# Low halves of the weights moved from GpSimd to VectorE, and the first two products behind four norms made row by row

## The chip, the cores and the metric

The kernel runs on one core of a Trainium2 chip. The time is device microseconds from start to end of one execution; the median of several runs is what two kernels are compared by. The profile is one further execution, recorded instruction by instruction. Engines are written as the profile writes them: PE is TensorE's matmuls, PEld its weight loads, DVE is VectorE, ACT is ScalarE, POOL is GpSimd, SP the queue that issues the DMAs.

## The reference, cut to what matters

Two blocks of two layers each, everything in fp32, 256 tokens of 1024 channels. The first block makes, in each layer, one wide input product and three branches (a Mamba-2 scan, a sliding-window attention, a forgetting attention), gates and adds them:

```
for layer in range(DEPTH):
    h = rms_norm(x, norm_w[layer])
    proj = jnp.einsum('bsd,de->bse', h, w_in[layer])
    ...
    x = x + jnp.einsum('bsd,de->bse', merged, w_out[layer])
return rms_norm(x, final_norm_w)
```

The second block has a second stream `xc` of 256 context tokens beside x, modulates each norm with a scale and a shift that come from a condition vector, and has a mixing half (attention, pooling, Fourier) and a feed-forward half:

```
h = modulate(rms_norm_2(x, norm_mix[l]), sh1, sc1)
... = jnp.split(h @ w_in[l], IN_SPLITS, axis=-1)
x = x + g1 * merge_branches(...)
hf = modulate(rms_norm_2(x, norm_ffn[l]), sh2, sc2)
x = x + g2 * conv_ffn(hf, w_up[l], conv_w[l], w_down[l])
```

In layer 0 of it both streams run (512 columns), in layer 1 the context stream needs only its keys and values.

## The kernel before

**An fp32 product as three products.** Each operand is split into a high part that PE takes exactly (`hi`, an ACT copy to fp32r) and a low part (`lo` = raw - hi). A product is hi·hi + hi·low + low·hi, three matmuls of 128x128 weights (lines 878 to 880 in `chan`, 891 to 893 in `toks` where the activations are the stationary side, 953 to 955 in `small`).

**The weights.** They stream from HBM by SP's queue in halves of 128x1024 into 7 buffers `raw`, and from there into a ring of 5 buffers `hi` and `lo` (`NS` = 5, line 15). A `split` of a half is two instructions: ACT makes `hi` (line 1239; it waits until PE has used the half five places back, `was("used", u.i - NS)`), then the subtraction makes `lo`, on DVE (line 1554) or on POOL (line 2021), after `hi`. Which one is decided in `plan`:

```
u.x = (w, len(rows), "dve" if u.i >= NS and u.i % (4 if u.x[0] else 2) == 1 else "pool")
```

The first flag of `u.x` is `self.share`: every second half goes to DVE in the forgetting-attention and convolution part of the first block, every fourth elsewhere, none of the first five.

**The order.** `Order` (line 196 on) writes one list of units by hand. Every engine walks through the same list and runs its own part of each unit in order, waiting on semaphores. `gemm` (line 265) makes a product of 8 rows k of 128 channels: `split_after(i, 0)` (the refill of the ring place that this product's first half frees), the product, `split_after(i, 1)`, then `tick`, which appends one step of each side work (attention, scan, mixing). A product of 256 columns by 256 tokens is 48 matmuls. In an `urgent` product the refills are put off: `early_split` and `late_splits` (lines 235 and 240) place them around the next norm.

**The norms.** A norm number t is: the squares on ACT summed on DVE into `t_SQA` (line 1564), a matmul with ones (916), a square root on ACT (1267), a reciprocal on DVE (1571), a matmul that spreads it over the partitions (923), and then the eight rows. In the first block (`norm1`) rows come in pairs: DVE scales into PSUM (1585), ACT copies to the high part (1278), DVE subtracts to the low part (1591). In the second block (`norm2`) per row: DVE (1850), for 512 columns DVE (1853) and ACT (1423), ACT makes the high part (1426), and the low part is made on DVE (1842) for even rows and on POOL (2051) for odd ones; in norms 3 and 8 on DVE for all. Each row of the product behind waits for its row of the norm, `at("h", u.l, k)`.

Norms and the first product behind each: 0 and 1 in the first block, `small` (128 columns) and then `q`; 3 in the second block's layer 0, `uf`; 4, the feed-forward of layer 0, `up`, one chunk whose two column groups of 128 by 512 tokens are two units; 5, layer 1, `uf` twice; 6, its feed-forward, `up` twice.

Of the kernel before, what the change touches and what calls it, by code (L numbers as in the profile page):

```python
# [144 lines left out]
class Unit:  # L145
# [9 lines left out]
    n: tuple = ()  # L155
    x: tuple = ()


class Order:
# [105 lines left out]
    def gemm(self, kind, l, c, fn, nkt, ncol, tw, urgent=False, x=(), then=None):  # L265
# [133 lines left out]
    def layer1(self, l):  # L399
# [11 lines left out]
        for g in range(4):  # L411
            for off, kind in ((O_QC, "q"), (O_KC, "k")):
# [89 lines left out]
    def block2(self, l):  # L502
# [67 lines left out]
        for pr in range(11):  # L570
            g, p2 = (pr + 1) // 2, (pr + 1) % 2
            for vg in range(2):
                self.gemm("up", l, pr, wcols("w_up_2", l, vg * DFF + np.arange(pr * 256, pr * 256 + 256)), 8, 256, tw,
                          x=(vg,), then=lambda m0: self.up_then(l, pr, vg, m0, tw))
# [267 lines left out]
def tensor(e, units, t, M):  # L842
# [25 lines left out]

    def chan(u, nkt, ncol, tw, xh, xl, point, *events):

        b = gbank(u)
        for k in range(nkt):
            q.wait_ge(point(k))
# [8 lines left out]

    def toks(u, nkt, ncol, c0, nc, xh, xl, blocks, point, part):

        b = gbank(u)
        for k in range(nkt):
            q.wait_ge(point(k))
            hi, lo = weights(u, k, ncol)
            for j, tb in enumerate(blocks):
# [54 lines left out]

    def of_h(u, *events):
        chan(u, 8, 256, 256, hh, hl, lambda k: at("h", u.l, k), *events)

    def small(u):
        b = gbank(u)
        for k in range(8):  # L950
            q.wait_ge(at("h", u.l, k))
# [127 lines left out]

    def uf(u):  # L1080
        z, nz = u.x
        toks(u, 8, 256, 0, 256, block(t.H2), block(t.HL2), (2 * z, 2 * z + 1),
             lambda k: at("h", 8 if u.l == 0 and z else 3 + 2 * u.l, k), z)

# [111 lines left out]
    todo = dict(rstd=rstd, rstdb=rstdb, mod=mod, mod2=mod2, q=of_h, k=of_h, conv=of_h, rope=of_h, z=of_h, gate=lambda u: of_h(u, ("gatemm", u.l)),  # L1196
                small=small, small4=small4, vc=vc, vb=vc, scores=scores, turn=turn, pv=pv, ssm0=ssm0, ssm3=ssm3, ssm4=ssm4,
                rope2=rope2, gn_sum=gn_sum, proj=proj, wout=wout, uf=uf, k2=k2, v2=v2, q2=lambda u: of_h2(u, 256 if u.l else 512),
                gate2=lambda u: of_h2(u, u.x[3]), rope2b=rope2b, pool1=pool1, four1=four1, mix2=mix2, pair0=pair0, pair3=pair3,
                pair4=pair4, proj2=proj2, wout2=wout2, up=ffup, down=down)  # L1200
    for u in units:
        if u.kind in todo:
            todo[u.kind](u)
# [333 lines left out]
def vector(e, units, t, M):  # L1537
# [296 lines left out]
    def norm2(u):  # L1834
# [175 lines left out]
def gpsimd(e, units, t, M):  # L2010
# [52 lines left out]
def plan():  # L2063
# [199 lines left out]
```

## Time and profile before

| | |
|---|---|
| median of 3 runs | 2189.99 us (2189.62 to 2190.36) |
| the profiled execution: its time, its span | 2188.52 us, 2186.8 us |
| PE busy | 2085.0 us, 95% |
| DVE busy | 1230.1 us, 56% |
| ACT busy | 1112.0 us, 51% |
| POOL busy | 959.3 us, 44% |
| `lo` on POOL, `lo` on DVE | 360 and 146 instructions |

The span is 1.7 us shorter than that execution's own time, and that time lies 1.5 us under the median of the runs. A matmul's record is longer than the step to the next one, since matmuls overlap; how fast PE goes is read from the steps between starts and from counts in a stretch. PE's granted clock is given as a share of its full rate: 1.00 is 2.4 GHz, 0.50 is 1.2 GHz.

### The profile page before, as it was taken

How to read it: one execution, taken by the hardware profiler on the slowest of the kernel's cores; microseconds unless marked ns; L12 is line 12 of the kernel's file. 1: busy time of each engine (PE TensorE's matmuls, PEld its weight loads, DVE VectorE, ACT ScalarE, POOL GpSimd, SP SyncE). 2: the span in 40 equal slices, each digit the busy share in tenths (PEclk: the TensorE clock that was granted, in tenths of full speed). 3: DMA queues.
4: the chain of work that ended last, by engine and by line, in shares of the span. 5: the costliest groups of instructions: out<-in, count | busy, mean ns of one | idle time of the engine just before them, and what ended most of it. 6: DMA issues, size and time to landing. Idle time of an engine off the chain costs nothing.

```text
span 2186.8 us, 36805 instructions
## 1 busy us (share of the span) xinstructions
PE 2085.0 (95%) x14870; PEld 1856.7 (85%) x14870; DVE 1230.1 (56%) x2034; ACT 1112.0 (51%) x1892; POOL 959.3 (44%) x424
## 2 busy tenths in 40 slices
PE   6999999999999999999999999999999989999997
PEld 6998998998898999988666876778888777898997
DVE  5577757345677655473464435455544546766565
ACT  5575476544585475554475233433333346645553
POOL 4655654653546555642112332323333233465662
PEclk9999999999999999999999999999999989999998
DMA  6454544565654544563212434333333333354551
GB/s 238 150 189 170 185 149 147 183 221 186 225 177 157 182 155 154 195 227 110 97 68 77 163 127 164 116 125 125 116 135 107 131 109 109 124 183 140 189 184 58
DMA packets 93321, 330.65 MB, mean 151 GB/s; under 512 B 10080, under 2 KB 13408, under 8 KB 92896
## 3 DMA queue, kind: packets, MB, share of 16 engines
q1 hardware_dynamic: 93152, 328.30, 43.6%
q8 instruction: 118, 1.93, 0.4%
q14 instruction: 51, 0.42, 0.1%
HBM read 327.08 MB, written 1.18 MB: 150 GB/s over the span
## 4 chain that ended last, share of the span: by engine, by line
PE 76%; DVE 11%; ACT 7%; issue 2%; DMA 2%; POOL 2%; SPq 0%; DVEq 0%; ACTq 0%; POOLq 0%
PE ps L878 21%; PE ps L879 21%; PE ps L880 21%; ACT t_hi L1239 2%; PE ps L932 2%; DVE t_lo L1554 1%; DMA t_A<-cu_scratch 1%; PE ps L891 1%; PE ps L892 1%; PE ps L893 1%; POOL t_lo L2021 1%; PE ps L1150 1%; DVE t_SQA L1564 1%; PE ps L1006 1%; PE ps L1160 1%
## 5 line engine op out<-in xcount | busy, mean ns | idle before, releaser
L2021 POOL TENSOR_TENSOR t_lo<-t_raw,t_hi 128x1024 fp32r<-128x1024 f32 (+1 forms) x360 | 884.9, 2468 | 1059.7 <-ACT t_hi L1239 1035.9
L878 PE MATMUL ps<-t_RB,t_hi 128*128 128x256 f32 (+1 forms) x3712 | 1170.8, 315 | 17.3 <-DVE t_RB L1842 5.3
L879 PE MATMUL ps<-t_RB,t_hi 128*128 128x256 f32 (+1 forms) x3712 | 1149.4, 310 | 0.0
L880 PE MATMUL ps<-t_RB,t_lo 128*128 128x256 f32 (+1 forms) x3712 | 1148.7, 309 | 0.0
L878 PEld LDWEIGHTS ps<-t_RB,t_hi 128*128 128x128 f32 x3712 | 712.3, 192 | 90.5 <-issue 31.5
L880 PEld LDWEIGHTS ps<-t_RB,t_lo 128*128 128x128 f32 x3712 | 712.6, 192 | 35.7
L879 PEld LDWEIGHTS ps<-t_RB,t_hi 128*128 128x128 f32 x3712 | 712.9, 192 | 34.9 <-issue 1.9
L1239 ACT ACTIVATE t_hi<-t_raw 128x1024 fp32r<-128x1024 f32 (+1 forms) x506 | 524.7, 1042 | 421.6 <-PE ps L880 387.9
L1554 DVE TENSOR_TENSOR t_lo<-t_raw,t_hi 128x1024 fp32r<-128x1024 f32 x146 | 211.2, 1447 | 264.4 <-ACT t_hi L1239 264.3
L1980 DVE SCALAR_TENSOR_TENSOR t_A<-ps,t_V,t_A 128x510 f32<-128x510 f32 (+1 forms) x176 | 102.2, 612 | 153.8 <-ACT t_A L1514 152.2
L1514 ACT ACTIVATE t_A<-ps,t_V 128x512 f32<-128x512 f32 (+1 forms) x88 | 48.5, 576 | 126.8 <-PE ps L880 126.8
L1953 DVE SCALAR_TENSOR_TENSOR t_X<-ps,t_MOD,t_X 128x256 f32<-128x256 f32 x168 | 72.1, 478 | 62.4 <-PE ps L880 62.4
L891 PE MATMUL ps<-t_hi,t_RB 128*128 128x256 f32 (+1 forms) x320 | 94.3, 295 | 4.3 <-DVE t_RB L1842 2.9
L892 PE MATMUL ps<-t_hi,t_RB 128*128 128x256 f32 (+1 forms) x320 | 91.5, 286 | 0.0
L893 PE MATMUL ps<-t_lo,t_RB 128*128 128x256 f32 (+1 forms) x320 | 91.5, 286 | 0.0
L891 PEld LDWEIGHTS ps<-t_hi,t_RB 128*128 128x128 f32 x320 | 62.9, 196 | 9.5 <-ACT t_E L1423 5.2
L1500 ACT ACTIVATE t_A<-ps 128x512 f32<-128x512 f32 (+1 forms) x48 | 22.4, 490 | 89.1 <-PE ps L880 85.9
L892 PEld LDWEIGHTS ps<-t_hi,t_RB 128*128 128x128 f32 x320 | 63.1, 197 | 0.4 <-issue 0.2
L893 PEld LDWEIGHTS ps<-t_lo,t_RB 128*128 128x128 f32 x320 | 63.0, 197 | 0.0
L1564 DVE TENSOR_TENSOR t_SQA<-t_SQA,t_NT 128x256 f32<-128x256 f32 (+1 forms) x63 | 47.5, 754 | 21.5 <-ACT t_NT L1260 18.0
L1526 ACT ACTIVATE t_RB<-t_A 128x512 fp32r<-128x512 f32 (+1 forms) x44 | 23.1, 526 | 70.5 <-DVE t_A L1995 70.5
L932 PE MATMUL ps<-t_raw,t_C 128*32 128x256 f32 x768 | 53.0, 399 | 2.6 <-DVE t_X L1953 2.6
(295 smaller groups left out, 2154.5 us busy)
## 6 DMA issues: line engine op xcount, KB each, us to landing
t_raw<-in_W SPq DMA_DIRECT2D x586, 512.0 KB, 3.5
t_A<-cu_scratch SPq DMA_DIRECT2D x8, 512.0 KB, 6.3
t_B<-cu_scratch SPq DMA_DIRECT2D x8, 512.0 KB, 4.4
t_raw<-in_W SPq DMA_DIRECT2D x16, 256.0 KB, 2.6
t_A<-in_C SPq DMA_DIRECT2D x2, 1536.0 KB, 6.8
t_X<-in_X SPq DMA_DIRECT2D x2, 512.0 KB, 4.4
t_X<-in_X SPq DMA_DIRECT2D x1, 1024.0 KB, 9.6
out<-t_X SPq DMA_DIRECT2D x1, 1024.0 KB, 4.8
```

The lines of the kernel that those rows point to most:

```text
L878: mm(o, hi[:, w], xh(k), start=k == 0 and j == 0, stop=False)
L879: mm(o, hi[:, w], xl(k), start=False, stop=False)
L880: i = mm(o, lo[:, w], xh(k), start=False, stop=k == nkt - 1 and m == u.x[1] - 1)
L891: mm(o, xh(k, tb), hi[:, w], start=k == 0 and j == 0, stop=False)
L892: mm(o, xl(k, tb), hi[:, w], start=False, stop=False)
L893: i = mm(o, xh(k, tb), lo[:, w], start=False, stop=k == nkt - 1 and tb == blocks[-1])
L932: i = mm(b[32 * j:32 * j + 32, 0:256], t.C32[:, k, :], t.raw[r % NR][:, j * 256:j * 256 + 256], start=k < 4, stop=k >= 4)
L1239: act(t.hi[s][:, 0:w], t.raw[r][:, 0:w], ACT.Copy).then_inc(*up("act", ("hi", u.i), ("split", u.i)))
L1554: tt(t.lo[s][:, 0:w], t.raw[r][:, 0:w], t.hi[s][:, 0:w].bitcast(F), ALU.subtract).then_inc(*up("dve", ("split", u.i)))
L1953: stt(out=x, in0=ps[:, z * 256:z * 256 + 256], scalar=t.modv(u.l, j, k, z), in1=x, op0=ALU.mult, op1=ALU.add).then_inc(*up("dve", ("x", s, ...
L1980: return stt(out=o[:, :, r], in0=ps[:, :, s], scalar=cw, in1=o[:, :, r], op0=ALU.mult, op1=ALU.add)
L2021: tt(t.lo[s][:, 0:w], t.raw[r][:, 0:w], t.hi[s][:, 0:w].bitcast(F), ALU.subtract).then_inc(*up("pool", ("split", u.i)))
```

## The change

Three edits. (1) `plan` sends every `lo` to DVE, all 506, the first five too; the low parts of all norm rows go to DVE, so POOL keeps only `fox_prep`, `ssm0` and `ssm2`. (2) A new `wide` unit takes the first two products behind norms 0, 1, 4, 5 and 6 and makes them row by row: for rows 0 to 5 first the one's matmuls, then the other's, and rows 6 and 7 at the end one after the other. Behind norms 0 and 1 these are `small` and `q` of group 0 (which stood one product later), behind 4 the two column groups of one `up` chunk, behind 5 the two `uf`, behind 6 the two `up`. The refills of the ring stand behind the `wide` unit. (3) In norms 5 and 6 one `early_split` more stands ahead of the reciprocal.

```
+    def wide(self, l, parts, tw):
+        group, chunks = [], []
+        for kind, c, fn, ncol, x, then in parts:
+            i = self.chunk(8 * ncol, fn)
...
+        self.add("wide", l=l, x=tuple(u for u, _, _ in group))
+        halves = [(i, h) for i in chunks for h in range(-(-self.width[i] // HF))]
+        self.split_after(*halves.pop(0))
+        for u, then, m0 in group:
...
+            self.units.append(u)
+            if halves:
+                self.split_after(*halves.pop(0))
@@ small
-        i = self.chunk(1024, small_cols(l))
-        self.split_after(i, 0)
-        self.add("small", l=l, i=i, g=(self.bank(),))
-        self.split_after(i, 1)
+        self.wide(l, [("small", 0, small_cols(l), 128, lambda m: (), None),
+                      ("q", 0, wcols("w_in", l, O_QC + np.arange(256)), 256, lambda m: (0, 2), None)], 256)
@@ block2, norm 5 (norm 6: if last)
+            self.early_split()
             b = self.rstd(t, (2, 1, 1))
@@ tensor
+    def wide(u):
+        for k in range(6):
+            for v in u.x:
+                led[v.kind](v, ks=(k,))
+        for v in u.x:
+            led[v.kind](v, ks=(6, 7))
@@ vector, norm2
-            if k % 2 == 0 or s in (3, 8):
+            if True:
@@ gpsimd, norm2
-        if s in (3, 8):
-            return
+        return
@@ plan
-            u.x = (w, len(rows), "dve" if u.i >= NS and u.i % (4 if u.x[0] else 2) == 1 else "pool")
+            u.x = (w, len(rows), "dve")
```

**DVE at norm 0**, the start of the program. Before:

```order
4 L1571 RECIPROCAL t_SM<-t_SM 128x2
5 L1585 SCALAR_TENSOR_TENSOR ps<-t_X,t_V,ps 128x256 x4
6 L1591 TENSOR_TENSOR t_RB<-ps,t_RB 128x512
7 L1585 SCALAR_TENSOR_TENSOR ps<-t_X,t_V,ps 128x256 x2
8 L1591 TENSOR_TENSOR t_RB<-ps,t_RB 128x512
9 L1585 SCALAR_TENSOR_TENSOR ps<-t_X,t_V,ps 128x256 x2
10 L1591 TENSOR_TENSOR t_RB<-ps,t_RB 128x512 x2
```

and now (lines of the new file stand 38 higher: 1592 is the `lo` subtraction, 1609 the reciprocal, 1623 and 1629 the norm's rows):

```order
4 L1592 TENSOR_TENSOR t_lo<-t_raw,t_hi 128x1024
5 L1609 RECIPROCAL t_SM<-t_SM 128x2
6 L1623 SCALAR_TENSOR_TENSOR ps<-t_X,t_V,ps 128x256 x4
7 L1629 TENSOR_TENSOR t_RB<-ps,t_RB 128x512
8 L1592 TENSOR_TENSOR t_lo<-t_raw,t_hi 128x1024
9 L1623 SCALAR_TENSOR_TENSOR ps<-t_X,t_V,ps 128x256 x2
10 L1629 TENSOR_TENSOR t_RB<-ps,t_RB 128x512
11 L1592 TENSOR_TENSOR t_lo<-t_raw,t_hi 128x1024
12 L1623 SCALAR_TENSOR_TENSOR ps<-t_X,t_V,ps 128x256 x2
13 L1629 TENSOR_TENSOR t_RB<-ps,t_RB 128x512
14 L1592 TENSOR_TENSOR t_lo<-t_raw,t_hi 128x1024
```

One `lo` stands ahead of the reciprocal now, and one between each two pairs of rows.

**PE behind norm 0.** Before, the last two rows k of `small` (953 to 955) and the first of `q`:

```order
21 L953 MATMUL ps<-t_RB,t_hi 128x256
22 L954 MATMUL ps<-t_RB,t_hi 128x256
23 L955 MATMUL ps<-t_RB,t_lo 128x256
24 L953 MATMUL ps<-t_RB,t_hi 128x256
25 L954 MATMUL ps<-t_RB,t_hi 128x256
26 L955 MATMUL ps<-t_RB,t_lo 128x256
27 L878 MATMUL ps<-t_RB,t_hi 128x256
28 L879 MATMUL ps<-t_RB,t_hi 128x256
29 L880 MATMUL ps<-t_RB,t_lo 128x256
```

and now, from the first row on (990 to 992 are `small`, 907 to 909 are `q`):

```order
3 L990 MATMUL ps<-t_RB,t_hi 128x256
4 L991 MATMUL ps<-t_RB,t_hi 128x256
5 L992 MATMUL ps<-t_RB,t_lo 128x256
6 L907 MATMUL ps<-t_RB,t_hi 128x256
7 L908 MATMUL ps<-t_RB,t_hi 128x256
8 L909 MATMUL ps<-t_RB,t_lo 128x256
9 L907 MATMUL ps<-t_RB,t_hi 128x256
10 L908 MATMUL ps<-t_RB,t_hi 128x256
11 L909 MATMUL ps<-t_RB,t_lo 128x256
12 L990 MATMUL ps<-t_RB,t_hi 128x256
```

Each row of the norm now feeds nine matmuls before PE asks for the next.

**DVE at norm 6**, the last feed-forward. Before:

```order
1478 L1564 TENSOR_TENSOR t_SQA<-t_SQA,t_NT 128x256 x2
1479 L1830 TENSOR_SCALAR t_S1S<-t_MOD 128x16
1480 L1832 TENSOR_TENSOR t_S1S<-t_S1S,t_V 128x16
1481 L1571 RECIPROCAL t_SM<-t_SM 128x2
1482 L1575 TENSOR_TENSOR t_RS<-t_C,t_SM 128x256
```

and now:

```order
1714 L1602 TENSOR_TENSOR t_SQA<-t_SQA,t_NT 128x256 x2
1715 L1868 TENSOR_SCALAR t_S1S<-t_MOD 128x16
1716 L1870 TENSOR_TENSOR t_S1S<-t_S1S,t_V 128x16
1717 L1592 TENSOR_TENSOR t_lo<-t_raw,t_hi 128x1024
1718 L1609 RECIPROCAL t_SM<-t_SM 128x2
1719 L1613 TENSOR_TENSOR t_RS<-t_C,t_SM 128x256
```

The refill of edit (3) stands between the sum of squares and the reciprocal.

## Rows read from the trace of the kernel before

**Rows 1.** The page: busy time of the engines.
```profile
PE 2085.0 (95%) x14870; PEld 1856.7 (85%) x14870; DVE 1230.1 (56%) x2034; ACT 1112.0 (51%) x1892; POOL 959.3 (44%) x424
```

**Rows 2.** Groups by line: busy us, mean ns | idle before, releasers.
```profile
L2021 POOL TENSOR_TENSOR t_lo<-t_raw,t_hi 128x1024 fp32r<-128x1024 f32 (+1 forms) x360 | 884.9, 2468 | 1059.7 <-ACT t_hi L1239 1035.9 <-PE ps L1160 8.1 <-PE ps L880 8.1
L1239 ACT ACTIVATE t_hi<-t_raw 128x1024 fp32r<-128x1024 f32 (+1 forms) x506 | 524.7, 1042 | 421.6 <-PE ps L880 387.9 <-PE ps L893 29.7 <-PE ps L955 3.3
L1554 DVE TENSOR_TENSOR t_lo<-t_raw,t_hi 128x1024 fp32r<-128x1024 f32 x146 | 211.2, 1447 | 264.4 <-ACT t_hi L1239 264.3
L1608 DVE TENSOR_TENSOR t_MOD<-t_MOD,t_V 128x4 f32<-128x4 f32 x48 | 34.7, 723 | 1.6
```

**Rows 3.** One line's durations, ns min/median/max.
```profile
L1608 DVE TENSOR_TENSOR t_MOD<-t_MOD,t_V x48: 161/164/2309, 119.3 to 1799.8; 128x4 f32<-128x4 f32 x48
```

**Rows 4.** PE's waits: us in total, times, longest us.
```profile
PE ps L916 <- DVE t_SQA L1564: 26.9, 8, 9.2
PE ps L1055 <- ACT t_B L1368: 5.9, 2, 4.1
...
PE ps L962 <- DVE t_E L1654: 4.8, 1, 4.8
...
PE ps L878 <- POOL t_lo L2021: 3.4, 2, 2.6
```

**Rows 5.** Timeline of DVE ahead of L962: start us, us, engine line.
```profile
40.68 2.52 DVE L1641 TENSOR_TENSOR t_T<-t_T 64x256 f32<-64x256 f32 x1
...
45.71 0.42 DVE L1645 SCALAR_TENSOR_TENSOR t_E<-t_T 64x256 f32<-64x256 f32 x1
```

**Rows 6.** Timeline of DVE at norm 0; in brackets idle before, releaser.
```profile
10.51 0.17 DVE L1571 RECIPROCAL t_SM<-t_SM 128x2 f32<-128x2 f32 x1 [1.40 <-ACT t_SM L1267]
12.72 1.66 DVE L1585 SCALAR_TENSOR_TENSOR ps<-t_X,t_V,ps 128x256 f32<-128x256 f32 x4 [2.04 <-PE ps L923]
...
17.92 0.69 DVE L1591 TENSOR_TENSOR t_RB<-ps,t_RB 128x512 fp32r<-128x512 f32 x1 [0.18 <-ACT t_RB L1278]
```

**Rows 7.** Timelines of DVE and of PE at norm 1.
```profile
497.61 2.03 DVE L1554 TENSOR_TENSOR t_lo<-t_raw,t_hi 128x1024 fp32r<-128x1024 f32 x1 [1.01 <-ACT t_hi L1239]
...
501.08 0.58 PE L953 MATMUL ps<-t_RB,t_hi 128*128 128x256 f32 x1 [2.78 <-DVE t_RB L1591]
```

**Rows 8.** Timelines of PE and of DVE at norm 4.
```profile
1358.90 0.47 PE L878 MATMUL ps<-t_RB,t_hi 128*128 128x512 f32 x1 [2.43 <-DVE t_RB L1842]
...
1370.93 0.47 PE L878 MATMUL ps<-t_RB,t_hi 128*128 128x512 f32 x1 [0.73 <-POOL t_RB L2051]
...
1359.43 1.30 DVE L1853 TENSOR_SCALAR t_E<-t_E,t_S1S,t_MOD 128x256 f32<-128x256 f32 x1
```

**Rows 9.** Stretches: us, busy of PE, PEld, DVE, ACT, POOL, PEclk, DMA.
```profile
46.00:53.00 7.00, 5.22 (x26) 5.11 (x27) 4.16 (x8) 0.00 (x0) 0.00 (x0) 0.51 0.51 174
496.60:506.80 10.20, 7.37 (x32) 7.07 (x33) 5.06 (x7) 4.24 (x6) 3.51 (x2) 0.50 0.62 243
1360.20:1367.00 6.80, 6.05 (x12) 3.32 (x12) 6.65 (x11) 4.73 (x8) 2.56 (x3) 0.50 0.23 92
1370.90:1377.80 6.90, 6.87 (x30) 5.74 (x31) 2.72 (x3) 2.63 (x4) 4.60 (x2) 1.00 0.38 127
...
1762.90:1773.20 10.30, 9.50 (x37) 7.83 (x36) 9.68 (x15) 7.26 (x13) 3.91 (x4) 0.50 0.00 0
```

**Rows 10.** Timeline of DVE at norm 6.
```profile
1973.73 0.17 DVE L1571 RECIPROCAL t_SM<-t_SM 128x2 f32<-128x2 f32 x1 [0.70 <-ACT t_SM L1267]
```

**Rows 11.** Two stretches of 50 us, columns as in Rows 9.
```profile
600.00:650.00 50.00, 50.00 (x438) 47.33 (x437) 37.42 (x82) 40.40 (x84) 23.49 (x12) 1.00 0.54 187
...
2000.00:2050.00 50.00, 50.00 (x419) 50.00 (x418) 34.49 (x61) 28.97 (x50) 32.23 (x14) 1.00 0.55 183
```

**Rows 12.** The chain that ended last; tile t_lo in 1070:1200 and in 1805:1895.
```profile
1138.56 1.22 DVE t_lo L1554
...
L2021 POOL TENSOR_TENSOR t_lo<-t_raw,t_hi x12: 1295/2366/2472, 1077.7 to 1198.9; 128x1024 fp32r<-128x1024 f32 x8, 128x512 fp32r<-128x512 f32 x4
...
L2021 POOL TENSOR_TENSOR t_lo<-t_raw,t_hi x15: 1264/2375/2429, 1808.3 to 1888.2; 128x1024 fp32r<-128x1024 f32 x10, 128x512 fp32r<-128x512 f32 x5
```

More of the change, by code:

```diff
@@ L156 @@
     x: tuple = ()
+    led: bool = False
 class Order:
@@ L284, in gemm @@
             self.mod_turn()
+    def wide(self, l, parts, tw):
+        group, chunks = [], []
+        for kind, c, fn, ncol, x, then in parts:
+            i = self.chunk(8 * ncol, fn)
+            chunks.append(i)
+            for m0 in range(0, max(1, ncol // 128), 512 // tw):
+                group.append((Unit(kind, l=l, c=c, i=i, g=(self.bank(),), x=x(m0), led=True), then, m0))
+        self.add("wide", l=l, x=tuple(u for u, _, _ in group))
+        halves = [(i, h) for i in chunks for h in range(-(-self.width[i] // HF))]
+        self.split_after(*halves.pop(0))
+        for u, then, m0 in group:
+            if then:
+                then(m0)
+            self.units.append(u)
+            if halves:
+                self.split_after(*halves.pop(0))
+        for i, h in halves:
+            self.split_after(i, h)
     def squares(self, t):
@@ L411, in layer1 @@
         for g in range(4):
-            for off, kind in ((O_QC, "q"), (O_KC, "k")):
+            for off, kind in ((O_QC, "q"), (O_KC, "k"))[not g:]:
                 self.gemm(kind, l, g, wcols("w_in", l, off + np.arange(g * 256, g * 256 + 256)), 8, 256, 256)
@@ L513, in block2 @@
             self.late_splits()
-            for c in range(2):
-                self.uf(l, c, self.uf_chunk(l, c), 0, True)
+            self.wide(l, [("uf", c, wcols("w_in_2", l, 768 + np.arange(c * 256, c * 256 + 256)), 256, lambda m: (0, 1), None)
+                          for c in range(2)], 256)
         else:
@@ L558, in block2 @@
         self.add("s1", l=l, x=(4, t + 1))
+        if last:
+            self.early_split()
         b = self.rstd(t + 1, (2, 1, 1))
@@ L571, in block2 @@
             g, p2 = (pr + 1) // 2, (pr + 1) % 2
-            for vg in range(2):
+            first = () if pr else range(512 // tw if last else 1)
+            if pr == 0:
+                self.wide(l, [("up", 0, wcols("w_up_2", l, vg * DFF + np.arange(256)), 256,
+                               lambda m, vg=vg: (m, min(2, m + 512 // tw), vg),
+                               lambda m, vg=vg: self.up_then(l, 0, vg, m, tw)) for vg in first], tw)
+                self.tick()
+                self.mod_turn()
+            for vg in range(len(first), 2):
                 self.gemm("up", l, pr, wcols("w_up_2", l, vg * DFF + np.arange(pr * 256, pr * 256 + 256)), 8, 256, tw,
@@ L867, in taken, with chan @@
             i.then_inc(*up("pe", ("used", u.i + k * ncol // HF), *events))
-    def chan(u, nkt, ncol, tw, xh, xl, point, *events):
+    def chan(u, nkt, ncol, tw, xh, xl, point, *events, ks=None):
         b = gbank(u)
-        for k in range(nkt):
+        for k in ks or range(nkt):
             q.wait_ge(point(k))
@@ L881, in chan, with toks @@
             taken(u, i, k, nkt, ncol, ("mm", u.i, u.x[0]), *events)
-    def toks(u, nkt, ncol, c0, nc, xh, xl, blocks, point, part):
+    def toks(u, nkt, ncol, c0, nc, xh, xl, blocks, point, part, ks=None):
         b = gbank(u)
-        for k in range(nkt):
+        for k in ks or range(nkt):
             q.wait_ge(point(k))
@@ L943, in mod2, with of_h, small @@
         i.then_inc(*up("pe", ("modt", u.l, u.c), ("mtr", u.l * 24 + u.c)))
-    def of_h(u, *events):
-        chan(u, 8, 256, 256, hh, hl, lambda k: at("h", u.l, k), *events)
-    def small(u):
+    def of_h(u, *events, ks=None):
+        chan(u, 8, 256, 256, hh, hl, lambda k: at("h", u.l, k), *events, ks=ks)
+    def small(u, ks):
         b = gbank(u)
-        for k in range(8):
+        for k in ks:
             q.wait_ge(at("h", u.l, k))
@@ L1078, in wout, with uf @@
         chan(u, 8, 256, 256, hh, hl, lambda k: at("m", u.l, k // 2), ("layer", u.l))
-    def uf(u):
+    def uf(u, ks=None):
         z, nz = u.x
         toks(u, 8, 256, 0, 256, block(t.H2), block(t.HL2), (2 * z, 2 * z + 1),
-             lambda k: at("h", 8 if u.l == 0 and z else 3 + 2 * u.l, k), z)
+             lambda k: at("h", 8 if u.l == 0 and z else 3 + 2 * u.l, k), z, ks=ks)
     def k2(u):
@@ L1196, in tensor @@
     todo = dict(rstd=rstd, rstdb=rstdb, mod=mod, mod2=mod2, q=of_h, k=of_h, conv=of_h, rope=of_h, z=of_h, gate=lambda u: of_h(u, ("gatemm", u.l)),
-                small=small, small4=small4, vc=vc, vb=vc, scores=scores, turn=turn, pv=pv, ssm0=ssm0, ssm3=ssm3, ssm4=ssm4,
+                wide=wide, small4=small4, vc=vc, vb=vc, scores=scores, turn=turn, pv=pv, ssm0=ssm0, ssm3=ssm3, ssm4=ssm4,
                 rope2=rope2, gn_sum=gn_sum, proj=proj, wout=wout, uf=uf, k2=k2, v2=v2, q2=lambda u: of_h2(u, 256 if u.l else 512),
@@ L1200, in tensor @@
                 pair4=pair4, proj2=proj2, wout2=wout2, up=ffup, down=down)
+    led = dict(small=small, q=of_h, uf=uf, up=ffup)
     for u in units:
-        if u.kind in todo:
+        if u.kind in todo and not u.led:
             todo[u.kind](u)
```

4 lines of the change are left out of this document (2 added, 2 removed).

## The prediction

> **What bounds the kernel now.** I read the page first: PE is busy 2085.0 us of a span of 2186.8 [rows 1], so all that can be won without fewer matmuls is the 101.8 us in which it is not, and what the lower clock costs. DVE has 957 us free, POOL is busy 44% [rows 1]. PE's steps go at 50 us / 419 = 0.119 us for 256 columns where nothing disturbs it [rows 11], and at 6.90 / 30 = 0.23 us for 512 [rows 9]. Then the waits of PE: 26.9 us in eight waits for the sum of squares, 5.9 for an ACT copy in attention, 4.8 in one wait for a small DVE chain, 3.4 for a `lo` of POOL [rows 4]. These are 41 of the 101.8; the other 61 are many short ones, those for rows of the norms (2.78, 2.43, 0.73 [rows 7, 8]) among them. So the list of waits has no large one that a slow `lo` causes: POOL has time for 360 of them at 2.47 us each [rows 2]. What the change can win lies elsewhere, in what POOL does to DVE.
>
> That is read from the spread of one form. L1608 works on 128x4, takes 0.164 us in the median and up to 2.309, with a mean of 0.723 [rows 2, 3]: an instruction of the smallest size lasts as long as a `lo` on POOL. `lo` on DVE has a mean of 1.447 [rows 2] where an undisturbed one takes 1.22 [rows 12], L1641 takes 2.52 at 40.68 and its neighbour L1645 of the same size 0.42 [rows 5], L1853 takes 1.30 [rows 8]. I read this as DVE being held until a running POOL instruction ends. The excess that has rows is 48 x 0.56 = 27 us and 146 x 0.22 = 33 us; there is more in other forms.
>
> The Trainium skill, "SBUF — State Buffer", section "Who interferes with whom", names such a mechanism: DVE and GpSimd share a port pair, an exclusive lock, which a DVE instruction with two SBUF inputs needs too. These stretched instructions agree; it doesn't say how often PE waits for the held one, and the sum below doesn't use it.
>
> **Part 1, all `lo` on DVE: the load.** 360 instructions at 1.22 [rows 12] add 439 us to DVE, less 60 for the excess above, so DVE's busy time comes out at 1230 + 439 - 60 = 1609 us at most. If every second removed instruction of POOL had held DVE for half of its 2.47 us, 222 us fall away instead of 60, and it is 1447. Both leave DVE under 75%. POOL keeps 64 instructions.
>
> **What contention gives back.** At L962 the held L1641 costs 2.52 - 0.42 = 2.1 us of the 4.8 [rows 4, 5] and others of that chain the rest: nothing (if `lo`s in DVE's queue take its place) to -4.8; I take the whole, since only short instructions stand in that chain. Behind it PE runs at a granted clock of 0.51, the lower level of 1.2 GHz: 26 matmuls in 7.00 us [rows 9], where at 0.119 they need 3.1. Had it not idled I take 3.5 of those 3.9 us as won too. Together **-8.3** (0 to -8.7). The two waits at L1055, 5.9 us, follow DVE work by way of ACT: **-3** (0 to -5.9). Of the remaining waits outside the norm rows, 61 - 21 = 40, a part is DVE being late by a held instruction; as the mean of `lo` on DVE shows 16% above an undisturbed one, and the small forms far more, I take a third, -12, with the 3.4 for POOL's `lo` in it (bounds 0 and -25): **-12**. The 26.9 for the sum of squares I leave: its chain of ACT squares, DVE sums, root and reciprocal is the same; only its DVE instructions can be held less, which the -25 covers.
>
> **What the queue costs.** A `lo` on DVE waits for its `hi` in order, and everything behind it (attention's, scan's and the norm's steps) waits with it. Before, 146 of these stood there and the idle time ahead of them was 264 us, all of it waiting for `hi` [rows 2]; DVE had that time. Now there are 3.5 times as many. Dense places are 600 to 650, where DVE is busy 37.42 us and POOL has 12 instructions [rows 11]: nine `lo`s more are 11 us, 48.4 of 50; and 2000 to 2050, 34.49 plus 14 x 1.22 = 51.6, less what contention gives back. In each of some three such stretches I let PE lose 2 to 3 us: **+8**. Bounds: 0, since the ring hides a `lo` that comes late by less than three halves (3 x 24 x 0.119 = 8.6 us), and +31, worked out under the rivals.
>
> **Part 2, norm by norm.** Norm 0: one `lo` ahead of the reciprocal, which had been idle 1.40 before 10.51 [rows 6]; the `hi` is there at about 10.1, so the `lo` ends at 11.3, 0.85 late. Between the pairs of rows stand three `lo`s more, 3.7 us, each behind an ACT `hi` of 1.04 [rows 2], 3.0 us more. The last low rows, ready at 17.92 + 0.69 = 18.6 [rows 6], come at 26.1. Before, three matmuls of `small` and 48 of `q` followed, to about 25.3; now 18 matmuls follow (2.2 us), to 28.3: **+2.9** (+0.8 if the `hi` are early, +6.6 if all rows wait for the fourth `lo` and the clock stays low).
>
> Norm 1: before, PE stood 2.78 us for a row because a `lo` of 2.03 us stood ahead of it [rows 7], and ran at 0.50, 32 matmuls in 10.20 us [rows 9]. Now the rows come about 1.7 us later (more `lo`s ahead), but the 24 matmuls of `small` no longer run alone and slowly: **-2.1** (-3.7 to 0).
>
> Norm 4: rows come every (1370.93 - 1358.90) / 7 = 1.72 us [rows 8], and a row feeds 3 x 0.23 = 0.69 us of work. PE waits in each. With the second unit in them it is 1.38 us, which still fits; of its 24 matmuls, 5.5 us behind the last row in the stretch from 1370.90 [rows 9], all but the last two rows' 6 are done by then: -4.1 at full clock. At 0.50, which 1360.2 to 1367 had [rows 9], 1.38 would be 2.76 and not fit. With L1853 no longer held (1.30 us [rows 8]) the rows themselves come faster. I take **-3.8** (-4.6 to -1.5). POOL's odd low rows, for which the wait of 0.73 was [rows 8], become 0.4 us on DVE each, inside the 1.72.
>
> Norm 5: 37 matmuls took 10.30 us at 0.50 [rows 9], 5.9 more than at 0.119. Two `uf` together bring 6 matmuls to each row; half of the loss goes, **-3.0** (-4.5 to -1). Norm 6: the early `lo`, behind a `hi` of 1.04, ends about 0.7 after the 1973.73 at which the reciprocal started [rows 10]; there PE is nearly bound by its own matmuls, so little comes back: **+0.5** (0 to +1). Part 3 is in these two. Norms together: +2.9 - 2.1 - 3.8 - 3.0 + 0.5 = **-5.5**.
>
> **The sum.** -5.5 - 8.3 - 3 - 12 + 8 = -20.8. Against the profiled execution's own 2188.5 that is 2167.7; the median of the runs is 1.5 above it, so 2169. Own range of this case: 2156 to 2182, since the bounds of the terms are independent and not all met together.
>
> **The rivals.** A, slower: DVE's queue becomes the bound in the attention stretches. In 1070 to 1200 POOL had 12 `lo`s, in 1805 to 1895 it had 15 [rows 12]; the chain that ended last already goes through a `lo` of DVE, 1.22 us at 1138.56 [rows 12]. If each of the 27 stands between two links of a chain that PE waits for, it costs 27 x 1.22 = 33 us, and the dense stretches 10 more than I let them: -21 + 33 + 10 = +22, or **2212**. It decides where a `lo` stands behind a `hi` that waits for PE while PE waits for a step queued behind that `lo`; from a lateness of the 8.6 us above also by starving the ring. Against it: 957 free us, and the gain per instruction no longer held. For it: 264 us of waiting for `hi` in DVE's queue at 146 of them. The Trainium skill, "Perfetto Trace Analysis", section "Optimizing Scalar/DVE Operations", has both sides of it: a saturated DVE may want work moved to GpSimd, yet the two share a port, so that it might not help. At 56% this DVE isn't saturated, so the first half would not bite unless locally.
>
> B, no change: what POOL held on DVE was time for which PE never waited, except at L962; there -8.3, norms -3 instead of -5.5, queue +8, the rest 0: -3, or **2187**. For it: PE's waits outside the norms are short and many. C, a larger gain: all held time was late work: -5.5 - 8.3 - 5.9 - 25 and no new queue waits: -44.7, or **2145**. For it: 27 and 33 us of excess in two forms alone.
>
> **How the numbers follow.** The forecast gets 0.60, A 0.16, B 0.12, C 0.12. A measurement of this kernel can tell about 0.2%, 4.4 us, from no change: faster is below 2185.6, slower above 2194.4. Faster: 0.60 + 0.12 = 0.72; same 0.12; slower 0.16. The range leaves out most of A and a part of C: 2147 to 2196.
>
> **What would show it.** In the profile after: POOL busy under 80 us; 506 `lo` with a mean near 1.2 us; L1608 (now 1646) with a maximum near its median; DVE between 1447 and 1609 us. The wait at L962 and the half clock behind it gone (contention); rows of norm 4 still 1.7 us apart or less, with six matmuls between; at norm 0 a last low row near 26 us. If A holds, PE shows long waits for attention's steps in 1070 to 1200 and 1805 to 1895, or for `t_lo` from DVE. I would be wrong if the small instructions keep their stretched maxima without POOL (then another cause held them), or if DVE's idle time ahead of `lo` becomes PE's wait.

## The result, and the profile after

The changed kernel takes 2153.19 us (median of 4 runs, 2151.65 to 2154.62) beside 2190.18 us for the kernel before (2189.62 to 2190.66): a ratio of 0.9831, 95% interval 0.9816 to 0.9845, or 37 us faster. Its profiled execution has a span of 2152.8 us, 34.0 less than before. The prediction was 2169, with 2147 to 2196 as the range: the direction was right, the gain larger than the 21 us forecast, and the result lies below the narrower 2156 to 2182 that its sum gave.

The page of the changed kernel, busy time of the engines, and its group for the low halves (busy us, mean ns | idle before, releasers), to be read against [rows 1, 2]:

```profile
PE 2074.8 (96%) x14870; PEld 1850.0 (86%) x14870; DVE 1377.1 (64%) x2406; ACT 1110.9 (52%) x1892; POOL 72.0 (3%) x52
...
L1592 DVE TENSOR_TENSOR t_lo<-t_raw,t_hi 128x1024 fp32r<-128x1024 f32 (+1 forms) x506 | 613.7, 1217 | 455.5 <-ACT t_hi L1277 447.5
```

DVE took over some 439 us of work (360 x 1.22) and is busy only 147 us longer: by this estimate some 290 us of its busy time before were no work. Its mean for a low half fell from 1447 to 1217 ns. The small form (one instruction with one shape) that led me to this, and a one-input form of 128x8, in the changed kernel (ns min/median/max):

```profile
L1646 DVE TENSOR_TENSOR t_MOD<-t_MOD,t_V x48: 161/163/391, 121.8 to 1771.0; 128x4 f32<-128x4 f32 x48
...
L1731 DVE TENSOR_SCALAR t_ST<-t_ST x16: 170/171/173, 65.3 to 810.3; 128x8 f32<-128x8 f32 x16
```

Before, the first went up to 2309 ns [rows 3], and the second was

```profile
L1693 DVE TENSOR_SCALAR t_ST<-t_ST x16: 171/1222/2403, 68.2 to 825.0; 128x8 f32<-128x8 f32 x16
```

PE's waits (us in total, times, longest), against [rows 4]:

```profile
PE ps L953 <- DVE t_SQA L1602: 23.0, 7, 9.2
PE ps L1059 <- DVE t_ST L1738: 8.4, 3, 4.0
PE ps L1187 <- DVE t_MOD L1646: 4.2, 3, 2.0
PE ps L1092 <- ACT t_B L1406: 4.1, 2, 2.6
...
PE ps L907 <- DVE t_lo L1592: 1.2, 1, 1.2
```

The 4.8 us at the small chain (L962, now L999) are gone, the 5.9 at L1055 (now L1092) are 4.1, and one wait has grown: L1059 for L1738, 8.4 us in three, which before was 2.9 in one. It is the mechanism of rival A, in one kind of place. The changed kernel's DVE there (start us, us, engine line, in brackets idle before and releaser), and PE behind it:

```profile
779.21 1.22 DVE L1592 TENSOR_TENSOR t_lo<-t_raw,t_hi 128x1024 fp32r<-128x1024 f32 x1 [5.03 <-ACT t_hi L1277]
...
780.95 1.21 DVE L1592 TENSOR_TENSOR t_lo<-t_raw,t_hi 128x1024 fp32r<-128x1024 f32 x1
782.08 0.68 DVE L1748 COPY t_B<-ps 128x512 f32<-128x512 f32 x1
782.68 0.15 DVE L1738 TENSOR_TENSOR t_ST<-t_ST 128x8 f32<-128x8 f32 x1
...
782.87 0.69 PE L1059 MATMUL ps<-t_B,t_A 128*64 128x256 f32 x2 [3.96 <-DVE t_ST L1738]
```

and the same step in the kernel before:

```profile
794.85 0.17 DVE L1700 TENSOR_TENSOR t_ST<-t_ST 128x8 f32<-128x8 f32 x1 [3.00 <-ACT t_ST L1334]
```

Before, the 0.17 us step ran as soon as ACT's last exponential was there. Now a low half stands ahead of it that waited 5.03 us for its high half (ACT made that only behind the same exponentials), and another behind that one.

The best view of where the time went is this table. All kernels run the same 14870 matmuls, so each stretch is cut by the number of the matmul that starts, and the figures are us more or less than the kernel before takes for the same stretch of matmuls (inside a `wide` unit the order differs; the cuts lie outside). It is worked out from the starts of PE's matmuls in the profiled executions. The columns are the kernels described below.

```
matmuls       before, us  what stands there        changed  wide_only  lo_dve  dve_only  pool_tiny  lag  lag_some
    0-100       9-28    norm 0, small, q             +3.4      +3.4     +9.2    +10.1      +0.9   +3.1    +3.6
  100-300      28-59    small chain (L962)           -7.1      -7.1     -7.1     -7.1      -6.9   -7.1    -7.1
  300-2100     59-278   forgetting attention on      -4.7      +6.2     -5.6     -5.5      -7.7   +5.0    -4.4
 2100-2500    278-327   sliding attention, layer 0   +3.3      -1.6     +5.4     +4.4      -1.3   -1.7    -1.7
 2500-3900    327-493                                -3.2      -2.8     -3.4     -3.4      -3.4   +0.9    -3.8
 3900-4350    493-555   norm 1                       -4.0      -3.5     +0.5     +1.5      -0.7   -4.0    -4.0
 4350-4600    555-591                                -6.9      -0.7     -6.4     -6.1      -6.9   -5.8    -6.8
 4600-6000    591-762                                -0.6      +0.3     -1.8     -0.3      -6.2   +3.0    -2.1
 6000-6450    762-815   sliding attention, layer 1   +7.1      +0.3     +6.9     +6.2       0.0   +1.0    +1.0
 6450-8200    815-1030                               -5.4      -3.7     -4.9     -4.1      -5.4   -5.4    -8.4
 8200-9750   1030-1338  pair attention, layer 0      +0.8      +4.4     -5.5     -4.0      -8.1   -5.2    -4.3
 9750-10000  1338-1391  norm 4                       -5.3      -4.1      0.0     -1.2       0.0   +1.3    -5.3
10000-11700  1391-1754  feed-forward                 -2.6      -2.6      0.0     -0.2      -0.1   -3.5    -2.7
11700-11900  1754-1793  norm 5                       -6.1      -4.7      0.0     -1.3      -0.2   -3.8    -5.6
11900-13000  1793-1934  pair attention, layer 1      -1.6      -0.1     -1.6     -1.6      -2.5   -4.9    -4.5
13000-14869  1934-2178  norm 6 to the end            -1.1      +2.5     -2.0     -1.8      -2.5   +0.3    -1.6
total                                               -34.0     -13.9    -16.6    -14.6     -51.0  -26.7   -57.7
```

The change touches five norms, 0, 1, 4, 5 and 6 (the title says four). Their stretches give -13.1, the small chain -7.1, the stretch behind 4350 -6.9 (it had 6.8 us at a granted clock of 0.50, half clock, from 572), and the two sliding attentions take 10.4 back: the waits at L1059, and with them 3.4 us (at 310) and 6.8 us (at 781) at half clock. Over the whole execution PE's idle time fell from 93.3 to 69.6 us, and the time at half clock from 91.4 to 63.4.

Norm 4 in the changed kernel: PE at the first row and two rows further on (start us, us), and one stretch (busy of PE, PEld, DVE, ACT, POOL, PEclk, DMA), against [rows 8, 9]:

```profile
1341.62 0.47 PE L907 MATMUL ps<-t_RB,t_hi 128*128 128x512 f32 x1 [2.42 <-DVE t_RB L1880]
...
1344.87 0.50 PE L907 MATMUL ps<-t_RB,t_hi 128*128 128x512 f32 x1
...
1342.00:1348.00 6.00, 6.00 (x24) 3.82 (x22) 5.85 (x12) 4.58 (x8) 0.00 (x0) 1.00 0.55 225
```

Rows now come (1344.87 - 1341.62) / 2 = 1.63 us apart, six matmuls fill them, PE is never idle, and the clock stays at 1.00 where it had fallen to 0.50. At norm 1:

```profile
487.00 0.35 PE L990 MATMUL ps<-t_RB,t_hi 128*128 128x256 f32 x1 [1.76 <-DVE t_RB L1629]
...
487.30:490.70 3.40, 3.40 (x18) 3.40 (x17) 2.61 (x4) 1.32 (x3) 0.00 (x0) 0.51 1.03 414
```

The lower clock still comes, behind the same wait of 1.76 us as before (it stands ahead of the first row in both kernels), but lasts 3.4 us where it was 10.2 [rows 9]; the wait of 2.78 [rows 7], which fell into those 10.2 us, is gone.

### The profile page after: what moved, and what is told of

The parts are those of the page before. It is cut to its first block, busy times and chain, and to the rows that moved or that the text cites. A ratio compares the mean times of both kernels' runs of the same rounds, so it can differ in the third digit from the quotient of the medians.

```text
span 2152.8 us, 36677 instructions
## 1 busy us (share of the span) xinstructions
PE 2074.8 (96%) x14870; PEld 1850.0 (86%) x14870; DVE 1377.1 (64%) x2406; ACT 1110.9 (52%) x1892; POOL 72.0 (3%) x52
## 4 chain that ended last, share of the span: by engine, by line
PE 84%; DVE 8%; ACT 6%; issue 1%; DMA 1%; SPq 0%; DVEq 0%; ACTq 0%
PE ps L907 23%; PE ps L909 22%; PE ps L908 22%; DVE t_lo L1592 3%; ACT t_hi L1277 2%; PE ps L920 2%; PE ps L921 2%; PE ps L922 2%; PE ps L969 2%; PE ps L1187 1%; PE ps L1208 1%; PE ps L1059 1%; PE ps L1197 1%; PE ps L1043 1%; DMA t_raw<-in_W 1%
## 5 line engine op out<-in xcount | busy, mean ns | idle before, releaser
L1592 DVE TENSOR_TENSOR t_lo<-t_raw,t_hi 128x1024 fp32r<-128x1024 f32 (+1 forms) x506 | 613.7, 1217 | 455.5 <-ACT t_hi L1277 447.5
L921 PE MATMUL ps<-t_hi,t_RB 128*128 128x256 f32 (+1 forms) x320 | 91.4, 286 | 0.0
L1298 ACT ACTIVATE t_NT<-t_X 128x256 f32<-128x256 f32 (+1 forms) x63 | 27.0, 458 | 39.1 <-DVE t_SQA L1602 15.6
L1800 DVE SCALAR_TENSOR_TENSOR t_A<-ps,t_V,t_A 128x255 f32<-128x255 f32 (+2 forms) x96 | 41.7, 476 | 4.4 <-ACT t_A L1343 3.3
```

What stands on the lines that cost most here:

```text
L921: mm(o, xl(k, tb), hi[:, w], start=False, stop=False)
L1592: tt(t.lo[s][:, 0:w], t.raw[r][:, 0:w], t.hi[s][:, 0:w].bitcast(F), ALU.subtract).then_inc(*up("dve", ("split", u.i)))
```

## The experiments

My theory was that POOL's instructions hold DVE and that this lateness reaches PE (theory 1); its rival, that the stretched instructions were waited for by nobody and the rows made together bring the gain (theory 2). All four kernels of the first group ran beside the kernel before at 2188.9 us.

**lo_dve**, the kernel before with

```
-            u.x = (w, len(rows), "dve" if u.i >= NS and u.i % (4 if u.x[0] else 2) == 1 else "pool")
+            u.x = (w, len(rows), "dve")
```

> The kernel before with one line changed: all 506 low halves on DVE, norm rows and order as before. Theory 1 (POOL's instructions hold DVE, and that lateness reaches PE): 2190 - 18 = 2172, with POOL under 100 us busy and L1608's maximum near its median; norm 0 some 3 us later. Theory 2 (the gain of the whole change comes from the rows made together, not from the low halves): no change, 2187 to 2192, since the stretched instructions were waited for by nobody and the queue of DVE gets longer.

Measured: 2171.79 us, ratio 0.9924 (0.9912 to 0.9937), 17 us faster. Theory 1's number. Norm 0 alone is 9.2 us longer in it.

**wide_only**, the changed kernel with the line above undone, and in `norm2` of DVE and POOL the low rows divided as before.

> The changed kernel with the low halves and the low rows divided between POOL and DVE as before: only the wide unit and the two early refills are left of the change. Theory 1: the norms alone, 5.5 to 15 us, 2175 to 2185 (in the traces the stretches around norms 1, 4, 5 and 6 are 3.3, 6.8, 6.1 and 2.2 us shorter, part of it by the low rows on DVE). Theory 2: nearly the whole gain, 2155 to 2160.

Measured: 2174.64 us, ratio 0.9932 (0.9918 to 0.9945), 14 to 15 us faster. Not the whole gain, but half of it is not at the norms: 7.1 us are at the small chain. There the cause is the order: q's 48 matmuls now stand ahead of L962, which finds its input ready though POOL works as before. So that wait has two cures, each enough by itself (lo_dve gains the same 7.1), and they don't add. From 300 to 2100 this kernel loses 6.2 us. PE waits for POOL's low halves in it:

```profile
PE ps L907 <- POOL t_lo L2059: 8.3, 4, 3.4
```

2.5 of these 8.3 us are at norm 0, and 5.8 in the stretch, where the kernel before has 3.4. That explains 2.4 of the 6.2; two parts at half clock, at 67 and 211, of 3.4 us each, which before are not there, explain some more, and the rest I haven't followed.

**dve_only**, both moves to DVE, no `wide`, no early refills.

> The kernel before with all low halves and all low rows of the norms on DVE, without the wide unit and without the two early refills. Theory 1: like the run with the low halves alone and 2 us less, 2170, since at norm 4 the waits for POOL's low rows go. Theory 2: within 2 us of the kernel before. If parts add up, this run's gain and that of the wide unit alone sum to 37 us.

Measured: 2171.44 us, ratio 0.9916 (0.9903 to 0.9930), 17 to 18 us faster: the norm's low rows on DVE by themselves give nothing that can be told from lo_dve (1.2 us at norm 4, 1.3 at norm 5 in the table, lost again at norm 0 and 1). With wide_only it sums to 32 or 33 of the 37. That isn't adding up, since the 7.1 us of the small chain are in both: without counting them twice the parts give 25, and the two together 12 more. By the table 10.1 of these are at norm 0 (+3.4 and +10.1 alone, +3.4 together).

**pool_tiny**, the kernel before, with POOL subtracting 8 columns of each low half from the eleventh half on (the other columns of `lo` are left as they were, so this kernel leaves out work that the product needs; it only prices):

```
+            v = w if u.i < 2 * NS else 8
-            tt(t.lo[s][:, 0:w], t.raw[r][:, 0:w], t.hi[s][:, 0:w].bitcast(F), ALU.subtract).then_inc(*up("pool", ("split", u.i)))
+            tt(t.lo[s][:, 0:v], t.raw[r][:, 0:v], t.hi[s][:, 0:v].bitcast(F), ALU.subtract).then_inc(*up("pool", ("split", u.i)))
```

> The kernel before, but from the eleventh half on POOL subtracts only 8 columns of each of its low halves; the rest of it is left out, and DVE does no more than before. It prices what POOL's instructions do to DVE without the load that goes to DVE instead. Theory 1: 2190 - 30 = 2160, and what is missing to that in the run with all low halves on DVE is the cost of DVE's queue (about 12 us). Theory 2: within 4 us of 2190.

Measured: 2137.28 us, ratio 0.9756 (0.9742 to 0.9770), 52 us faster, well beyond the 30 I had written. Its busy times, and the small form:

```profile
PE 2070.8 (97%) x14870; PEld 1847.8 (87%) x14870; DVE 967.1 (45%) x2034; ACT 1112.2 (52%) x1892; POOL 176.8 (8%) x424
...
L1608 DVE TENSOR_TENSOR t_MOD<-t_MOD,t_V x48: 161/163/166, 111.2 to 1753.7; 128x4 f32<-128x4 f32 x48
```

DVE does the same work in 263 us less. Part of the 52 can be that the low halves are ready sooner (before, PE waited 3.4 us for them [rows 4]); that nearly all of it is DVE is borne out by pool_dummy below. Then putting the 360 low halves on DVE costs at most 52 - 17 = 35 us, which I had put at 8. The columns show where: norm 0 (+9.2 against +0.9), the sliding attentions (+5.4 and +6.9 against -1.3 and 0.0), 4600 to 6000, and the pair attention.

The second group ran beside the kernel before at 2188.8 us. Two kernels put POOL to work again in the changed kernel, for nobody, at the 360 places of before:

```
+        elif not (u.i >= NS and u.i % (4 if u.x[3] else 2) == 1):
+            w = u.x[0]
+            q.wait_ge(at("hi", u.i), was("used", u.i - NS), M.last("pool"))
+            tt(DUM(w), DUM(w), DUM(w), ALU.subtract).then_inc(*up("pool"))
```

and pool_memset with `e.memset(DUM(w), 0.0)` in the last line. `DUM(w)` is w columns of a buffer of its own, at most 704. Lines stand one higher here than in the changed kernel.

> The changed kernel with work on POOL that nobody needs: at each of the 360 places where POOL made a low half before, it subtracts a buffer of 704 columns from itself (two inputs and the output in SBUF, about 0.69 of the length of a low half). DVE, ACT and PE do what they do in the changed kernel. Theory 1 (POOL's running instructions hold DVE): 0.69 of the 52 us that the run with 8-column low halves gained, 35 us, so 2153 + 35 = 2188; L1646 (128x4) has again a maximum above 1 us. Rival (what was won came from the low halves being ready earlier, or from the fuller queue of DVE being better ordered): within 4 us of 2153.

> The same, but POOL only writes: a memset of 704 columns at each of the 360 places. The Trainium skill, SBUF — State Buffer, section Who interferes with whom, lets a DVE instruction with two SBUF inputs contend only with a GpSimd instruction that reads SBUF. If that holds here: within 4 us of 2153 and L1646's mean below 0.2 us. If any running instruction of POOL holds DVE: the same 0.69 x 52 us scaled by the length of a memset, 2165 or more.

Measured: pool_dummy 2201.93 us, ratio 1.0062 (1.0040 to 1.0084); pool_memset 2148.51 us, ratio 0.9821 (0.9802 to 0.9841). The one costs 49 us against the changed kernel, the other nothing that can be told. One small line of DVE and POOL's added line, ns min/median/max, in pool_dummy:

```profile
L1647 DVE TENSOR_TENSOR t_MOD<-t_MOD,t_V x48: 161/164/1346, 122.0 to 1813.7; 128x4 f32<-128x4 f32 x48
...
L2064 POOL TENSOR_TENSOR t_DUM<-t_DUM x361: 1039/2131/3630, 10.5 to 2172.9; 128x704 f32<-128x704 f32 x175, 128x512 f32<-128x512 f32 x6
```

and in pool_memset, with the one-input form of 128x8:

```profile
L1647 DVE TENSOR_TENSOR t_MOD<-t_MOD,t_V x48: 161/164/387, 121.5 to 1763.3; 128x4 f32<-128x4 f32 x48
...
L1732 DVE TENSOR_SCALAR t_ST<-t_ST x16: 170/172/734, 65.5 to 805.4; 128x8 f32<-128x8 f32 x16
...
L2064 POOL MEMSET t_DUM<- x361: 524/687/695, 10.5 to 2112.1; 128x704 f32 x175, 128x512 f32 x6
```

This settles theory 1: nothing waits for these instructions, all other engines do the same work, and those that read SBUF bring the stretched instructions and the time back. POOL's own remaining work isn't the cause: DVE waits for it 3.6 us in place of 2.2, PE never. Why it is 49 and not the 35 expected isn't shown; DVE has 360 more two-input subtractions to be held here than in the kernel before, and is busy 1588.5 us in place of 1377.1. It holds both ways: POOL's own 704 columns took 1358 ns at least and up to 3630.

The Trainium skill, "SBUF — State Buffer", section "Who interferes with whom", says that a DVE instruction with two SBUF inputs contends only with a GpSimd instruction that reads SBUF. The pair agrees: L1647, with two inputs, goes up to 1346 ns beside the one and to 387 beside the other, no more than the 391 it has without either. The memset is shorter, 0.69 us, and only one L1647 starts while one runs, so the better proof is a count over all forms. I call an instruction held if it is over 60 ns longer than the shortest of its form in the changed kernel, and take those of DVE that start while an added instruction of POOL runs with over 100 ns to go and that meet no other of POOL's:

```
DVE reads                        beside subtractions   beside memsets
two SBUF inputs (TENSOR_TENSOR)     232 of 240 held      0 of 89
one SBUF input (TENSOR_SCALAR)       11 of 11            2 of 4
an input in PSUM                      0 of 283           0 of 85
```

So the two-input instructions are held by the one kind and not by the other, and some one-input TENSOR_SCALAR by both. Instructions of DVE that read PSUM are not held even in the kernel before:

```profile
L1953 DVE SCALAR_TENSOR_TENSOR t_X<-ps,t_MOD,t_X x168: 469/476/486, 1311.4 to 2170.3; 128x256 f32<-128x256 f32 x168
```

**probs_first** and **lag** ask what the low halves cost in DVE's queue. probs_first puts, on DVE alone, the step behind an attention group's exponentials ahead of the refills that stood before it. lag holds each refill's subtraction back on DVE until the next one comes:

```
+        if held and (u.kind in ("split", "wide", "rstd", "norm1", "norm2", "plain") or u.i is not None and held.i < u.i + 3):
+            split(held)
+            held = None
+        if u.kind == "split" and u.i >= 12:
+            held = u
+        elif u.kind in todo:
...
```

> The changed kernel with another order on DVE at 16 places only: the step behind the exponentials of an attention group (L1738 and what follows) stands ahead of the two refills that stood before it. Theory 1a: the loss at 2100 to 2500 and 6000 to 6450 (by the number of the matmul; the waits at L1059 for L1738) goes, 2153 - 10 = 2143, and the wait at L1059 falls from 8.4 to under 2 us. Rival 1b: the wait only moves to the low halves, within 4 us of 2153.

Measured: 2150.75 us, ratio 0.9830 (0.9812 to 0.9849): no difference to the changed kernel. The wait at L1059 has moved to the copy that stands behind the low halves:

```profile
PE ps L1059 <- DVE t_B L1748: 6.2, 2, 3.7
```

So the small step was not alone in standing behind them, and moving it alone was the wrong cure.

> The changed kernel with one thing moved: on DVE alone, each subtraction of a low half from the thirteenth on stands one half later in the queue (ahead of the next one, or of the norm or product that needs it), so that its high half is there when DVE comes to it. Theory 1a (what the low halves cost in DVE's queue is the waiting for their high halves, 448 us of idle DVE time, with the small steps of attention behind it): the losses at the two scores stretches (3.3 and 7.1 us) and in the pair attention (3.7) go, 2153 - 12 = 2141. Rival 1b (the cost is the 1.22 us of each itself): within 4 us of 2153.

Measured: 2162.50 us, ratio 0.9884 (0.9868 to 0.9901), 9 us slower than the changed kernel, against both expectations. The table shows why neither fits: in the sliding and pair attentions it gains 5.0, 6.1, 6.0 and 3.3 us on the changed kernel, and loses elsewhere, 9.7 in 300 to 2100, 6.6 at norm 4. DVE's idle time ahead of the low halves, and PE's waits for the weights of the modulation products:

```profile
  ACT t_hi L1277: 159.5, 91
...
PE ps L969 <- DMA t_raw<-in_W: 13.8, 6, 4.6
```

The waiting of DVE fell from 447.5 to 159.5 us, and PE waits 13.8 us for DMAs where the changed kernel has 1.6. A raw buffer is loaded again once its low half is made (`load` in `sync` waits for `split` of seven rows before), so a low half made later starts a later load. These waits are at norm 1 (3.8 us), at 967 (3.1), at norm 4 (5.5) and ahead of norm 5 (1.4), so they explain the loss at norm 4. They don't explain the largest, 300 to 2100: there PE waits for no DMA, but 8.7 us for small steps of DVE and ACT in place of 2.6, and runs 10.2 us at half clock, at 132 and 204. That gave the next kernel, which holds back only where lag gained.

**lag_some**, the same holding back only while the sliding attention and the pair attention run (a flag set in `layer1` and `block2`), and **lag_norm0**, which also makes norm 0 as before, with the first five low halves on POOL. The kernel before took 2190.0 us beside them.

> The changed kernel with the low halves one half later in DVE's queue only in four stretches: the sliding-window attention of both layers of the first block and the pair attention of both layers of the second. Theory 1a (small steps of attention stand behind a low half that waits for its high half; delaying all low halves won there, and lost elsewhere because a low half made later frees its raw buffer and so the DMA of the next one later): the gains of those stretches without the losses, 2153 - 15 = 2138, with PE's waits for the DMA of t_raw under 5 us. Rival 1b (one wait only takes the place of another): 2150 to 2160.

Measured: 2132.04 us, ratio 0.9740 (0.9726 to 0.9753), 58 us faster than before and 21 faster than the changed kernel. The waits at L1059 are gone from the list (under 2.5 us), and what PE waits for the DMA of `t_raw` is

```profile
PE ps L974 <- DMA t_raw<-in_W: 0.6, 2, 0.4
```

It gains more than in its four stretches (-5.0, -6.1, -5.1, -2.9): 6450 to 8200 came 3 us shorter too. DVE keeps all its 1376 us of work, so the cost of the queue was mostly its order, not its load.

> The same, and norm 0 as in the kernel before: the first five low halves on POOL, small and q of group 0 one after the other. In the traces the stretch of the first 100 matmuls is 3.4 us longer in the changed kernel, 3.4 us longer with the wide unit and POOL's low halves, and 9.2 us longer with the low halves on DVE and no wide unit. Expected: 3 us below the run before it in this list, 2135. Rival: the order of small and q is what the small chain behind it needed, and the wait of 4.8 us at L962 comes back, 2 to 4 us above it.

Measured: 2130.07 us, ratio 0.9727 (0.9713 to 0.9741). This is the fastest kernel here, but the 2 us to lag_some lie within the intervals; in the traces norm 0 takes 2.2 us less, and the chain behind it still gains its 7.1, so the rival has fallen.

**no_early**, the changed kernel without the two early refills.

> The changed kernel without the two early refills at norms 5 and 6. Theory 1: worth 0 to 3 us, 2153 to 2156, since the refill would then stand behind the rows of the norm and the wide unit would wait for nothing else. Rival (the refill ahead of the reciprocal delays the norm): 2 us faster, 2151.

Measured: 2159.71 us, ratio 0.9864 (0.9850 to 0.9878), 6.5 us slower than the changed kernel, more than I thought. In the traces it is at norm 5, where the stretch is 0.2 us over the kernel before in place of 6.1 under it; from norm 6 on it differs by 0.1. PE's wait there:

```profile
PE ps L917 <- DVE t_lo L1589: 3.3, 1, 3.3
```

The second `uf` can't be made together with the first while its weights are still to be split behind the norm.

## Why the prediction was right, and where not

**The number.** 2153 lies in the range, but two errors of opposite sign are behind it, and that they cancelled is luck. In the stretches of the five norms the forecast was -5.5 and the traces give -13.1; in all others it was -15.3 (contention -23.3, queue +8) and they give -20.9. That is 7.6 and 5.6 of the 16 us by which the forecast was too cautious; the rest is that the medians lie 37 us apart and the profiled executions 34.

**Contention: the right mechanism, the size wrong.** I had -8.3 at the small chain, -3 at L1055 and -12 elsewhere, -23.3 in all. pool_tiny, where POOL lets go and DVE gets nothing in exchange, gains 52, and pool_dummy, which gives it back, loses 49. The small chain was close (-7.1), though in the changed kernel `wide` alone would have given it too (wide_only), which I hadn't seen; the wait at L1055 gave 1.8. The third of 40 us that I took for all other waits was the weak term: I sized it by the mean of the low half (1447 ns over 1220 is 19% more, not 16%), which is 1.22 us long and so hides most of a hold, and counted only waits. Small forms have holds of several times their length (0.16 us becomes 2.31), and behind many waits stands a stretch at 1.2 GHz: before, 267 of the matmuls started in such a stretch, in the changed kernel 199, in pool_tiny 145. In pool_tiny PE's idle time is 36.8 us less than before (56.5 against 93.3) and the time at half clock 35.6 less (55.8 against 91.4), worth at most half of that by my estimate, 18: together they cover the 51 of its trace. The bound of 1447 us that I gave for DVE's busy time failed for the same reason; 1377.1 was measured.

**The queue: +8 predicted, 35 measured**, as the difference between pool_tiny and lo_dve. Some 10 of these are in the stretches of the norms, which I had priced apart; the other 24 are three times the +8, and inside the bound of +31. (That bound was said to be worked out under the rivals, but what stands there is 8 + 33 + 10 = 51.) Rival A was a true account of the mechanism, too high in size, and wrong in the place: pair attention of layer 0, where 1070 to 1200 lies, is 0.8 us longer than before (8.9 longer than in pool_tiny), that of layer 1 1.6 shorter than before (0.9 longer than in pool_tiny), while the sliding attentions lost 10.4 us. It didn't decide because the other term was twice my size too: the two errors, of 29 and 27 us, nearly cancelled.

**The norms: -5.5 predicted, -13.1 in the traces.** Norm 0: +2.9 against +3.4, but by another way: the last low row ends at 26.4, as worked out (26.1), while without the wide unit it is +9.2 (lo_dve); there `wide` is what keeps the low halves' cost down, which I hadn't seen. With POOL's low halves it costs the same 3.4. Norm 1: -2.1 against -4.0, since the wait of 2.78 went and the clock rose sooner. Norm 4: -3.8 against -5.3; I had feared that the lower clock stays, and it didn't come at all. Norm 5: -3.0 against -6.1, and I hadn't seen on which edit it rests: without the early refill the rows made together gain nothing there (+0.2 in no_early), and I had passed over that edit with "Part 3 is in these two". The early refill without `wide` was not run. Norm 6 with what follows: +0.5 against -1.1; the reciprocal came 0.5 us later behind the squares, near the 0.7 said, and nothing came of it.

**The last low row at norm 0** in the changed kernel, the one row that the prediction named a time for:

```profile
25.73 0.68 DVE L1629 TENSOR_TENSOR t_RB<-ps,t_RB 128x512 fp32r<-128x512 f32 x1
```

**What stays open.** Single stretches move by 2 to 5 us between kernels that don't differ there (8200 to 9750: -5.5 in lo_dve, +0.8 in the changed kernel; 10000 to 11700: -2.7 in lag_some, -6.7 in lag_norm0; norm 5 behind it: -5.6 and +0.8). The stretches shift against each other, and I haven't separated that. That later low halves delay the loads is read from lag's waits for DMAs, and no kernel with another buffer for `raw` was run. The 35 us of the queue are a difference of two kernels, and in pool_tiny the low halves are also ready sooner, so they are an upper value.

## What to carry to other kernels

Look at the spread of the shortest form on DVE: if its maximum is as long as an instruction of POOL, DVE may be held by it, and letting POOL do eight columns in place of a thousand shows whether it is and what it costs. When work moves into an in-order queue, price first what it waits for there and who stands behind it, not its own length: here 360 instructions of 1.22 us cost up to 35 us, and moving them by one place in four stretches, with the same work, brought 21 us back. But who makes something later also frees its inputs later: moved everywhere, the same instructions cost 9 us more than not moved at all. So such a move belongs only where a trace shows that it gains.

## What the runs showed of the hardware

Two-input subtractions in SBUF on POOL and on DVE hold each other for whole instructions: 0.16 us became 2.31, and POOL's 704 columns took 1.36 us at least, 2.13 in the median and up to 3.63. One-input TENSOR_SCALAR instructions of DVE in fp32 were held as well: L1693, 128x8, up to 2403 ns before and 173 at most afterwards. Instructions that read PSUM were not held: 168 of them between 469 and 486 ns, and in the kernel before none of the 44 such forms of DVE (with four instructions or more) spreads by more than 19 ns. POOL's memsets held no two-input instruction (0 of 89) and a few of the small one-input ones, 128x8 once (734 ns) and 128x2 up to 551, where it takes 173 at most in the changed kernel. What idle time of PE costs is not its length alone: at norm 1 the clock fell behind a wait of 1.76 us in both kernels, and stayed at 0.50 for 10.2 us before, with waits of 0.39 and 2.78 following, and for 3.4 us at 0.51 in the changed kernel, where none followed.
